# Query and key halves of the odd mixer with both input parts as one moving operand

## The chip, the core and the metric

The program runs on one core of one Trainium2 chip. Its time is the device time of one execution in microseconds (us). PE is the matmul engine, ACT the scalar engine, DVE the vector engine, POOL the GpSimd engine, SP the engine that issues the weight loads. The matmul engine's granted clock is 1.00 of its full 2.4 GHz in every stretch quoted here.

## What is computed

Three transformer-like blocks on 256 tokens of width 1024 in fp32, with a feed-forward part between the mixers. The change lies in the odd mixer, a banded attention of 16 heads of width 64:

```python
def odd_mixer(h, w_in, w_out, rel_bias):
    q, k, v = jnp.split(h @ w_in, 3, axis=-1)
    ...
    return chunk_band_attention(q, k, v, rel_bias) @ w_out
...
        s = jnp.einsum('bqhd,bkhd->bhqk', qblk.astype(jnp.float32), kb) * scale + bias[None]
        p = masked_softmax(s, valid[None, None, None, :])
        return jnp.einsum('bhqk,bkhd->bqhd', p, vb)
```

At 256 tokens a query sees its own chunk of 64 and all chunks before it, so a head's scores are one 256 x 256 matrix, kept as 128 x 128 for the first token tile and 128 x 256 for the second.

## The kernel before

fp32 products are made from two fp32r parts. A weight unit (256 columns of a weight, 128 x 2048 numbers in the buffer) is loaded by SP into one of three raw buffers; ACT writes its high part (L456, w_hi), DVE the rest (L1719, w_lo); both lie in six slots. The load of unit n waits until DVE has made the low part of unit n-3. The input, turned to have its channels on the partitions, lies in t_both as [channels, 8 k-tiles, 2 parts, 256 tokens]: t_hi and t_lo. A product is w_hi x t_hi + w_hi x t_lo + w_lo x t_hi (`three`, L1078 to L1080).

The odd mixer has 12 units of its input weight, n0 to n0+11: four for the values, which run first as pairs (`first_four`), and eight for queries and keys. Each of these eight gives two **halves** of 128 channels, one for two heads: half i belongs to group g = i // 4 of four heads, kind = i % 2 says query or key, and c = i % 4 // 2 which half of the unit. Before the change two halves of a unit (i and i+2) share a PSUM bank, 256 columns each, in banks 2 * (g % 2) + kind. ACT copies each half to q or k (L882, queries times 0.125) and counts qk_kept.

The order is written out by hand. On PE round i is: half i; at i = 8 and 12 `group_turn`, which turns the scaled output of the finished group of four heads (L1375, waits for o_ready); scores of head i-2 (L1349 and L1350, into bank 4; they wait for nmax_ok of the head before, and for POOL's padded query, L959); turn of the probabilities of head i-3 (L1358); values of head i-4 (L1366 to L1368). DVE makes the row maxima with the bias added (`maxima`, L1984), and at i = 8 and 12 `group_out`, which takes the reciprocal of the sums (L1993), multiplies (L2149) and counts o_ready. ACT makes the exponentials (`exps`, L644) and copies the turned probabilities (`keep_pt`, L636). Between these stand the splits of the weight units: `split_to(m)` makes the splits of all units below m that are still open. Every engine works through its own list in order, so an instruction that waits holds up all behind it. After the sixteen rounds `rows` multiplies with the output weight.

The feed-forward stage already has the form that the change brings to the halves: `by_channels_wide` (L1156 and L1160) takes both parts of t_both as one moving operand of 512 columns, so that w_hi x t_hi lands in the left and w_hi x t_lo in the right half of a bank, w_lo x t_hi is added to the left, and the two are added outside PE.

Of the kernel before, what the change touches and what calls it, by code (L numbers as in the profile page):

```python
# [16 lines left out]
ALU = mybir.AluOpType  # L17
ACT = mybir.ActivationFunctionType
AX = mybir.AxisListType

P = 128
S = 256
T = S // P
# [40 lines left out]
def build(nc, a, out, phases):  # L64
    stack = ExitStack()
    with stack:
# [3 lines left out]
        def sem(name):  # L70
            return stack.enter_context(nc.semaphore(name))
# [28 lines left out]
        def wv(at, *shape):  # L100
            n = int(np.prod(shape))
            v = ws[:, at:at + n]
            if len(shape) == 1:
                return v
            names = "abcd"[:len(shape)]
            return v.rearrange(f"p ({' '.join(names)}) -> p {' '.join(names)}",
                               **{c: s for c, s in zip(names, shape)})
# [35 lines left out]
        for ph in phases:  # L143
# [58 lines left out]
            else:  # L202
                q, k, v = wv(2304, 8, S), wv(4352, 8, S), wv(6400, T, D)
                bias = wv(8448, 4, 256)
                V = dict(bias=bias, q=q, k=k, o=[wv(2304 + 512 * g, T, 256) for g in range(4)])

                def reversed_bias(h, t):

# [63 lines left out]
        half_used = sem("half_used")  # L272
        last_half = sem("last_half")
        first_half_done = sem("first_half_done")
        qk_kept = sem("qk_kept")
        f_T = sem("f_T")
        dve_step = sem("dve_step")
# [107 lines left out]
        def half_of(ph, i):  # L385

            g, kind, c = i // 4, i % 2, i % 4 // 2
            return ph["n0"] + 4 + 2 * g + kind, 2 * (g % 2) + kind, g, kind, c

        ACT_CT, ACT_PE, DVE_PE = 1, 3, 2  # L390
        SINGLES = 11
# [48 lines left out]
        def _(act):  # L440
# [17 lines left out]
            def split_to(n):  # L458
                while cur[0] < min(n, N_UNITS):
                    split_hi(cur[0], widths.get(cur[0], UC))  # L460
                    cur[0] += 1
# [403 lines left out]
            def mix_odd(ph):  # L865
                V, n0 = ph["views"], ph["n0"]
                L = V["L"]
                split_to(n0 + 6)
                keep_unit(ph, 0)
                keep_unit(ph, 2)  # L870
                split_to(n0 + 7)
                keep_unit(ph, 1)
                split_to(n0 + 8)
                keep_unit(ph, 3)
                split_to(n0 + 10)
                for i in range(16):
                    n, b, g, kind, c = half_of(ph, i)
                    if c:
                        act.wait_ge(unit_used, n + 1)
                    else:  # L880
                        act.wait_ge(first_half_done, 2 * g + kind + 1)
                    nc.scalar.activation(V["qk"[kind]][:, 2 * g + c, :], bank[b][:, c * S:(c + 1) * S], ACT.Copy,  # L882
                                         scale=1.0 if kind else 0.125).then_inc(qk_kept, 1)
                    if i >= 8 and i % 4 == 0:
                        group_hi(i // 4 - 2, 6 + i // 4 % 2)
                    if i >= 3:
                        keep_pt(L, i - 3)
                    if i >= 2:
                        exps(L, i - 2)
                    if i >= 3 and i % 4 in (3, 0):  # L890
                        split_to(n0 + 11 + i // 2 - 1)
                keep_pt(L, 13)
                exps(L, 14)
                exps(L, 15)
                group_hi(2, 6)
                keep_pt(L, 14)
                keep_pt(L, 15)
                split_to(ph["after"] + 2)
                group_hi(3, 7)
                split_to(ph["after"] + 3)  # L900
# [168 lines left out]
        def _(pe):  # L1069
# [79 lines left out]
            def by_channels_wide(n, b, turn=0):  # L1149

                pe.wait_ge(lo_done, n + 1 + turn * SLOTS)
                wh, wl = w_cols(n)
                for c in range(2):
                    o, cs = bank[b + c], slice(c * P, (c + 1) * P)
                    for k in range(KT):
                        mm = nc.tensor.matmul(o[:, :], wh[:, k, cs], t_both[:, k, :, :].rearrange("p a s -> p (a s)"),  # L1156
                                              start=k == 0, stop=k == KT - 1)
                        if k == 0:
                            for j in range(KT):
                                nc.tensor.matmul(o[:, 0:S], wl[:, j, cs], t_hi[:, j, :], start=False, stop=False)  # L1160
                mm.then_inc(unit_used, 1)

            def pair_cols(w, n, k, width=UC):

# [341 lines left out]
            def mix_odd(ph):  # L1506
                V, n0 = ph["views"], ph["n0"]
                L = V["L"]
                first_four(ph, (0, 2), (1, 3))
                lo0 = seen[id(t_lo_ok)]  # L1510

                def half(i):
                    n, b, g, kind, c = half_of(ph, i)
                    pe.wait_ge(lo_done, n + 1)
                    if c:
                        pe.wait_ge(qk_kept, 4 * g + kind + 1)
                    elif g < 2:
                        pe.wait_ge(bank_free[b], ph["left"][ph["bank"].index(b)])
                    else:
                        pe.wait_ge(qk_kept, 4 * (g - 2) + 3 + kind)  # L1520
                    wh, wl = w_cols(n)
                    for k in range(KT):
                        mm = three(bank[b][:, c * S:(c + 1) * S], wh[:, k, c * P:(c + 1) * P], wl[:, k, c * P:(c + 1) * P],
                                   t_hi[:, k, :], t_lo[:, k, :], k == 0, k == KT - 1)
                    mm.then_inc(unit_used if c else first_half_done, 1)

                def scores(h):
                    pe.wait_ge(qk_kept, 4 * (h // 4) + 2 * (h % 4 // 2) + 2)
                    head_scores(L, h)

                def values(h):
                    if h >= 8 and h % 4 == 0:
                        pe.wait_ge(t_lo_ok, lo0 + h // 4 - 1)
                    head_values(L, h)

                def turn(h):
                    head_turn(L, h)

                def rows(u, t, rs=range(2)):
                    group_rows(ph, lo0, u, t, rs)  # L1540

                for i in range(16):
                    half(i)
                    if i >= 8 and i % 4 == 0:
                        group_turn(V["o"][i // 4 - 2], 6 + i // 4 % 2)
                    if i >= 2:
                        scores(i - 2)
                    if i >= 3:
                        turn(i - 3)
                    if i >= 4:  # L1550
                        values(i - 4)
                pe.wait_ge(qk_kept, 14)
                rows(0, 0, (0,))
                scores(14)
                turn(13)
                values(12)
                rows(0, 0, (1,))
                scores(15)
                values(13)
                rows(1, 0, (0,))  # L1560
                group_turn(V["o"][2], 6)
                turn(14)
                rows(1, 0, (1,))
                turn(15)
                values(14)
                pe.wait_ge(qk_kept, 16)
                rows(0, 1, (0,))
                values(15)
                rows(0, 1, (1,))
                rows(2, 0, (0,))  # L1570
                group_turn(V["o"][3], 7)
                rows(2, 0, (1,))
                rows(3, 0)
                rows(1, 1)
                rows(2, 1)
                rows(3, 1, (0,))
                turn_x(ph["next"], 0)
                rows(3, 1, (1,))
                nx(t_lo_ok, 4)
# [114 lines left out]
        def _(dve):  # L1694
# [582 lines left out]
            def mix_odd(ph):  # L2277
                V, n0 = ph["views"], ph["n0"]
                L = V["L"]

                split_to(n0 + 10)
                dve.wait_ge(bias_set, 1)
                for i in range(2, 16):
                    if i >= 8 and i % 4 == 0:
                        group_out(L, i // 4 - 2, V["o"][i // 4 - 2], 6 + i // 4 % 2)
                    maxima(L, i - 2)
                    if i >= 8 and i % 4 == 0:
                        group_lo(i // 4 - 2, 6 + i // 4 % 2)
                    if i >= 4 and i % 4 in (0, 1):
                        split_to(n0 + 11 + (i - 1) // 2 - 1)  # L2290
                group_out(L, 2, V["o"][2], 6)
                maxima(L, 14)
                maxima(L, 15)
                group_lo(2, 6)
                split_to(n0 + 17)
                group_out(L, 3, V["o"][3], 7)
                split_to(ph["after"] + 2)
                group_lo(3, 7)
                split_to(ph["after"] + 3)
# [80 lines left out]
```

## Time and profile before

| | us |
|---|---|
| median of 3 runs | 1323.35 (1323.13 to 1323.44) |
| the profiled execution | 1324.39 |
| its span | 1322.6 |
| PE busy | 1306.3 (99%) |
| DVE busy | 828.0 (63%) |
| ACT busy | 682.9 (52%) |

The profile describes one execution. Its span runs from the first to the last instruction; the time of that execution has 1.8 us more around it, and is 1.04 above the median. Times within the trace are counted from the span's start. The matmul durations that the rows give overlap, since matmuls are pipelined; the distance of two starts is what one costs.

### The profile page before, as it was taken

To read this page: it belongs to the slowest core of one execution; us is meant where nothing else is said; L and a number is where in the kernel's file an instruction comes from. 1 tells how busy PE (TensorE), PEld (TensorE's weight loads), DVE (VectorE), ACT (ScalarE), POOL (GpSimd) and SP (SyncE) were. 2 spreads that over 40 slices of the span, in tenths; PEclk is the share of its full clock that TensorE was granted. 3 is DMA by queue.
4 is the path that set the end of the run, shared out by engine and by line. 5 is a ranking of instruction groups with operands and counts; after the bars stand their busy time and mean duration, and the time that the engine had idled before them with its cause. 6 is when DMAs were issued, how large, how long until landed. Compare 5 with 4: busy or idle time off the path is not lost.

```text
span 1322.6 us, 18723 instructions
## 1 busy us (share of the span) xinstructions
PE 1306.3 (99%) x7310; PEld 1134.6 (86%) x7310; DVE 828.0 (63%) x992; ACT 682.9 (52%) x912; POOL 136.7 (10%) x162
## 2 busy tenths in 40 slices
PE   8999999999999999999999999999999999999998
PEld 7988888888888887888888888888888998888886
DVE  6997755565655558777765556665565545665553
ACT  6776544453544445556554445444454665554441
POOL 2770000000000001112100000000001441000000
PEclk9999999999999999999999999999999999999999
DMA  8334775553755545326575554675553744465540
GB/s 280 128 112 144 242 251 191 190 192 112 254 206 189 186 122 160 96 96 217 186 233 190 190 191 139 212 254 190 190 191 135 236 127 132 160 209 190 191 156 32
DMA packets 174352, 234.98 MB, mean 178 GB/s; under 512 B 4351, under 2 KB 154127, under 8 KB 174288
## 3 DMA queue, kind: packets, MB, share of 16 engines
q1 hardware_dynamic: 170368, 223.52, 50.7%
q0 software_dynamic: 3184, 9.37, 2.3%
q10 hardware_dynamic: 736, 1.19, 0.2%
q8 instruction: 45, 0.74, 0.2%
q14 instruction: 19, 0.16, 0.0%
HBM read 233.03 MB, written 1.05 MB: 177 GB/s over the span
## 4 chain that ended last, share of the span: by engine, by line
PE 92%; DVE 5%; DMA 2%; ACT 1%; issue 1%; POOL 0%; SPq 0%; DVEq 0%; ACTq 0%
PE psum L1156 22%; PE psum L1078 15%; PE psum L1080 15%; PE psum L1079 15%; PE psum L1160 12%; DVE w_lo L1719 2%; PE psum L1121 2%; PE psum L1120 2%; PE psum L1119 2%; PE psum L1350 1%; DMA raw<-in_w_in 1%; PE psum L1358 1%; PE psum L1248 1%; PE psum L1349 1%; PE psum L1367 1%; PE psum L1368 1%
## 5 line engine op out<-in xcount | busy, mean ns | idle before, releaser
L1719 DVE TENSOR_TENSOR w_lo<-raw,w_hi 128x2048 fp32r<-128x2048 f32 (+1 forms) x209 | 480.8, 2306 | 91.7 <-ACT w_hi L456 90.5
L456 ACT ACTIVATE w_hi<-raw 128x2048 fp32r<-128x2048 f32 (+1 forms) x212 | 402.6, 1905 | 40.6 <-PE psum L1080 11.2
L1156 PE MATMUL psum<-t_both,w_hi 128*128 128x512 f32 x1280 | 327.5, 393 | 0.0
L1156 PEld LDWEIGHTS psum<-t_both,w_hi 128*128 128x128 f32 x1280 | 230.2, 189 | 41.0
L1078 PE MATMUL psum<-w_hi,f_hi 128*128 128x512 f32 x488 | 192.8, 395 | 0.0
L1080 PE MATMUL psum<-w_hi,f_lo 128*128 128x512 f32 x488 | 190.2, 390 | 0.0
L1079 PE MATMUL psum<-w_lo,f_hi 128*128 128x512 f32 x488 | 190.1, 389 | 0.0
L1160 PEld LDWEIGHTS psum<-t_both,w_lo 128*128 128x128 f32 x1280 | 174.6, 190 | 12.3
L1160 PE MATMUL psum<-t_both,w_lo 128*128 128x256 f32 x1280 | 178.5, 282 | 0.0
L1078 PE MATMUL psum<-w_hi,t_both 128*128 128x512 f32 (+2 forms) x464 | 167.4, 361 | 2.8 <-DVE g_row L1959 2.7
L1080 PE MATMUL psum<-w_hi,t_both 128*128 128x512 f32 (+2 forms) x464 | 163.1, 351 | 0.0
L1079 PE MATMUL psum<-w_lo,t_both 128*128 128x512 f32 (+2 forms) x464 | 162.9, 351 | 0.0
L558 ACT ACTIVATE ws<-psum 128x512 f32<-128x512 f32 x40 | 24.0, 599 | 259.7 <-PE psum L1156 259.7
L1882 DVE TENSOR_TENSOR ws<-psum,ws 128x512 f32<-128x512 f32 x40 | 27.7, 692 | 199.6 <-ACT ws L558 199.6
L929 POOL TENSOR_TENSOR st<-st,minus_half 128x1 f32<-128x1 f32 (+3 forms) x35 | 27.3, 779 | 1016.6 <-DVE st L1766 756.4
L1080 PEld LDWEIGHTS psum<-w_hi,f_lo 128*128 128x128 f32 x488 | 91.6, 188 | 19.3
L1079 PEld LDWEIGHTS psum<-w_lo,f_hi 128*128 128x128 f32 x488 | 91.7, 188 | 18.1
L1078 PEld LDWEIGHTS psum<-w_hi,f_hi 128*128 128x128 f32 x488 | 91.7, 188 | 18.1
L1078 PEld LDWEIGHTS psum<-w_hi,t_both 128*128 128x128 f32 x464 | 88.4, 191 | 15.7 <-DVE g_row L1959 3.1
L1080 PEld LDWEIGHTS psum<-w_hi,t_both 128*128 128x128 f32 x464 | 88.4, 190 | 11.7
L1079 PEld LDWEIGHTS psum<-w_lo,t_both 128*128 128x128 f32 x464 | 88.6, 191 | 10.5
L1078 PE MATMUL psum<-t_both,w_hi 128*128 128x256 f32 x192 | 55.6, 290 | 1.4 <-ACT ws L882 0.8
(190 smaller groups left out, 1473.8 us busy)
## 6 DMA issues: line engine op xcount, KB each, us to landing
raw<-in_ffn_wg SPq DMA_DIRECT2D x44, 1024.0 KB, 5.5
raw<-in_ffn_wu SPq DMA_DIRECT2D x44, 1024.0 KB, 5.2
raw<-in_ffn_wd SPq DMA_DIRECT2D x44, 1024.0 KB, 5.0
raw<-in_even_w_in SPq DMA_DIRECT2D x12, 1024.0 KB, 5.1
raw<-in_odd_w_in SPq DMA_DIRECT2D x12, 1024.0 KB, 5.3
raw<-in_w_gate SPq DMA_DIRECT2D x11, 1024.0 KB, 5.5
raw<-in_w_up SPq DMA_DIRECT2D x11, 1024.0 KB, 5.3
raw<-in_w_down SPq DMA_DIRECT2D x11, 1024.0 KB, 4.9
```

Source lines behind the costliest of these rows:

```text
L456: nc.scalar.activation(w_hi[:, n % SLOTS, 0:w], raw[:, n % RAWS, 0:w], ACT.Copy).then_inc(hi_done, 1)
L929: nc.gpsimd.tensor_tensor(v, v, minus_half[:, 0:1].broadcast_to([P, v.shape[1]]), ALU.pow).then_inc(rstd_ready, 1)
L1078: nc.tensor.matmul(o, lh, rh, start=start, stop=False)
L1079: nc.tensor.matmul(o, lh, rl, start=False, stop=False)
L1080: return nc.tensor.matmul(o, ll, rh, start=False, stop=stop)
L1119: nc.tensor.matmul(out, t_hi[:, k, ts], wh(k), start=k == 0, stop=False)
L1120: nc.tensor.matmul(out, t_lo[:, k, ts], wh(k), start=False, stop=False)
L1121: return lambda: [nc.tensor.matmul(out, t_hi[:, k, ts], wl(k), start=False, stop=k == KT - 1) for k in range(KT)]
L1156: mm = nc.tensor.matmul(o[:, :], wh[:, k, cs], t_both[:, k, :, :].rearrange("p a s -> p (a s)"), start=k == 0, stop=k == KT - 1)
L1160: nc.tensor.matmul(o[:, 0:S], wl[:, j, cs], t_hi[:, j, :], start=False, stop=False)
L1719: nc.vector.tensor_tensor(w_lo[:, n % SLOTS, 0:w], raw[:, n % RAWS, 0:w], w_hi[:, n % SLOTS, 0:w].bitcast(F32), ALU.subtract).then_inc(lo_ ...
L1882: nc.vector.tensor_tensor(halves(f_s[:, b, :]), halves_of(4)[0], f_b[:, 0, :, :], ALU.add).then_inc(gate_sum, 1)
```

## The change

`half` on PE no longer calls `three` for each of eight k-tiles on 256 columns. It calls the new `by_channels_half`, which is the body of `by_channels_wide` for one c: one matmul of 512 columns with w_hi over t_both for k = 0, then eight of 256 columns with w_lo over t_hi, then seven more of 512. The half now fills a whole bank, so half i uses bank i % 4. Halves 0 to 3 wait for the bank to be left by the values; from half 4 on they wait for half i-4 to be kept.

ACT no longer writes q or k. It copies the right half of the bank into one of two buffers of 256 columns (in `masks`, whose tables aren't needed any more) and counts qk_part; from i = 2 on it waits until DVE has used that buffer. DVE adds: `whole(i)` waits for qk_part, takes the left half of the bank times 0.125 or 1 plus the buffer, writes q or k and counts qk_kept.

The weight splits at the start move. ACT made those of n0+8 and n0+9 before round 0, and makes them after the copies of halves 0 and 1. DVE made those up to n0+9 before the first maxima; now that of n0+7 stands behind the sum of half 0, that of n0+8 behind the sum of half 2, that of n0+9 behind the sum of half 3.

```diff
@@ half_of
-            return ph["n0"] + 4 + 2 * g + kind, 2 * (g % 2) + kind, g, kind, c
+            return ph["n0"] + 4 + 2 * g + kind, i % 4, g, kind, c
@@ ACT, mix_odd
-                split_to(n0 + 10)
                 for i in range(16):
...
-                    nc.scalar.activation(V["qk"[kind]][:, 2 * g + c, :], bank[b][:, c * S:(c + 1) * S], ACT.Copy,
-                                         scale=1.0 if kind else 0.125).then_inc(qk_kept, 1)
+                    if i >= 2:
+                        act.wait_ge(qk_kept, i - 1)
+                    nc.scalar.activation(V["part"][:, i % 2, :], bank[b][:, S:2 * S], ACT.Copy, scale=1.0 if kind else 0.125).then_inc(qk_part, 1)
+                    if i < 2:
+                        split_to(n0 + 9 + i)
@@ PE
+            def by_channels_half(n, b, c):
+
+                wh, wl = w_cols(n)
+                o, cs = bank[b], slice(c * P, (c + 1) * P)
+                for k in range(KT):
+                    mm = nc.tensor.matmul(o[:, :], wh[:, k, cs], t_both[:, k, :, :].rearrange("p a s -> p (a s)"),
+                                          start=k == 0, stop=k == KT - 1)
+                    if k == 0:
+                        for j in range(KT):
+                            nc.tensor.matmul(o[:, 0:S], wl[:, j, cs], t_hi[:, j, :], start=False, stop=False)
+                return mm
@@ PE, mix_odd, half
-                    if c:
-                        pe.wait_ge(qk_kept, 4 * g + kind + 1)
-                    elif g < 2:
+                    if i < 4:
                         pe.wait_ge(bank_free[b], ph["left"][ph["bank"].index(b)])
                     else:
-                        pe.wait_ge(qk_kept, 4 * (g - 2) + 3 + kind)
-                    wh, wl = w_cols(n)
-                    for k in range(KT):
-                        mm = three(bank[b][:, c * S:(c + 1) * S], wh[:, k, c * P:(c + 1) * P], wl[:, k, c * P:(c + 1) * P],
-                                   t_hi[:, k, :], t_lo[:, k, :], k == 0, k == KT - 1)
-                    mm.then_inc(unit_used if c else first_half_done, 1)
+                        pe.wait_ge(qk_kept, i - 3)
+                    by_channels_half(n, b, c).then_inc(unit_used if c else first_half_done, 1)
@@ DVE, mix_odd
-                split_to(n0 + 10)
+                def whole(i):
+
+                    n, b, g, kind, c = half_of(ph, i)
+                    dve.wait_ge(qk_part, i + 1)
+                    nc.vector.scalar_tensor_tensor(out=V["qk"[kind]][:, 2 * g + c, :], in0=bank[b][:, 0:S], scalar=1.0 if kind else 0.125,
+                                                   in1=V["part"][:, i % 2, :], op0=ALU.mult, op1=ALU.add).then_inc(qk_kept, 1)
+
+                split_to(n0 + 7)
+                whole(0)
+                split_to(n0 + 8)
+                whole(1)
                 dve.wait_ge(bias_set, 1)
                 for i in range(2, 16):
+                    whole(i)
+                    if i < 4:
+                        split_to(n0 + 7 + i)
                     if i >= 8 and i % 4 == 0:
                         group_out(L, i // 4 - 2, V["o"][i // 4 - 2], 6 + i // 4 % 2)
                     maxima(L, i - 2)
```

DVE's list at the start of the odd mixer, from the last instruction of the stage before (L1805), before the change. The names: w_lo is a split, ws,st<-psum,ws the maxima of one token tile, and each is followed by a short read of its accumulator.

```order
L1805 TENSOR_TENSOR t_both<-psum,t_both 128x4x128 [waits t_hi_ok] x2
L1719 TENSOR_TENSOR w_lo<-raw,w_hi 128x2048 [waits hi_done] x6
L1984 ISA ws,st<-psum,ws 128x128 [waits bias_in0,s_done,bias_set]
L1984 ISA st 128x1
L1984 ISA ws,st<-psum,ws 128x256
L1984 ISA st 128x1
```

The same place after the change; ws<-psum,masks is the sum of a half.

```order
L1721 TENSOR_TENSOR w_lo<-raw,w_hi 128x2048 [waits hi_done] x3
L2287 SCALAR_TENSOR_TENSOR ws<-psum,masks 128x256 [waits qk_part]
L1721 TENSOR_TENSOR w_lo<-raw,w_hi 128x2048 [waits hi_done]
L2287 SCALAR_TENSOR_TENSOR ws<-psum,masks 128x256 [waits qk_part]
L2287 SCALAR_TENSOR_TENSOR ws<-psum,masks 128x256 [waits qk_part,bias_set]
L1721 TENSOR_TENSOR w_lo<-raw,w_hi 128x2048 [waits hi_done]
L1986 ISA ws,st<-psum,ws 128x128 [waits bias_in0,s_done]
L1986 ISA st 128x1
L1986 ISA ws,st<-psum,ws 128x256
L1986 ISA st 128x1
L2287 SCALAR_TENSOR_TENSOR ws<-psum,masks 128x256 [waits qk_part]
L1721 TENSOR_TENSOR w_lo<-raw,w_hi 128x2048 [waits hi_done]
```

The block of six splits ahead of the first maxima is broken up. Sums of halves 0 to 3 stand in it, and the last two splits stand each between a sum and the maxima of heads 0 and 1.

DVE's list around round 8, before the change: L1993 and L2149 are the output of the first group.

```order
L1984 ISA ws,st<-psum,ws 128x128 [waits bias_in1,p_done,s_done]
L1984 ISA st 128x1
L1984 ISA ws,st<-psum,ws 128x256
L1984 ISA st 128x1
L1993 RECIPROCAL st<-st 128x8 [waits o_done]
L2149 TENSOR_TENSOR ws<-psum,st 128x512 [waits dve_step]
L1984 ISA ws,st<-psum,ws 128x128 [waits bias_in2,p_done,s_done]
```

The same place after the change (L1995 and L2151 are those two).

```order
L1986 ISA ws,st<-psum,ws 128x128 [waits bias_in1,p_done,s_done]
L1986 ISA st 128x1
L1986 ISA ws,st<-psum,ws 128x256
L1986 ISA st 128x1
L2287 SCALAR_TENSOR_TENSOR ws<-psum,masks 128x256 [waits qk_part]
L1995 RECIPROCAL st<-st 128x8 [waits o_done]
L2151 TENSOR_TENSOR ws<-psum,st 128x512 [waits dve_step]
L1986 ISA ws,st<-psum,ws 128x128 [waits bias_in2,p_done,s_done]
```

The output of the group stood behind the maxima of head 5 alone, and now the sum of half 8 stands between them.

PE's list at the end of half 8, before the change: the group's turn is L1375.

```order
L1078 MATMUL psum<-t_both,w_hi 128x256
L1079 MATMUL psum<-t_both,w_hi 128x256
L1080 MATMUL psum<-t_both,w_lo 128x256
L1375 MATMUL psum<-ident,ws 128x128 [waits o_ready]
L1375 MATMUL psum<-ident,ws 128x128 x3
L1349 MATMUL psum<-ws 128x128 [waits qz_ok,nmax_ok,qk_kept]
L1350 MATMUL psum<-ws 128x256
L1358 MATMUL psum<-ident,ws 128x128 [waits pt_kept,p_done]
```

And after it, where the turn is L1383:

```order
L1164 MATMUL psum<-t_both,w_hi 128x512 [waits qk_kept,lo_done]
L1168 MATMUL psum<-t_both,w_lo 128x256 x8
L1164 MATMUL psum<-t_both,w_hi 128x512 x7
L1383 MATMUL psum<-ident,ws 128x128 [waits o_ready]
L1383 MATMUL psum<-ident,ws 128x128 x3
L1357 MATMUL psum<-ws 128x128 [waits qz_ok,nmax_ok,qk_kept]
L1358 MATMUL psum<-ws 128x256
L1366 MATMUL psum<-ident,ws 128x128 [waits pt_kept,p_done]
```

The turn of the group keeps its place behind half 8, with its wait for o_ready; the half has become sixteen matmuls.

## Rows read from the trace of the kernel before

**Rows 1.** The page: chain that ended last, by engine.

```profile
PE 92%; DVE 5%; DMA 2%; ACT 1%; issue 1%; POOL 0%; SPq 0%; DVEq 0%; ACTq 0%
```

**Rows 2.** Stretch of the halves: us, then PE, PEld, DVE, ACT, POOL busy (instructions).

```profile
1033.17:1097.90 64.73, 63.95 (x523) 62.53 (x522) 30.94 (x67) 39.42 (x87) 29.88 (x43) 1.00 0.58 176
```

**Rows 3.** Waits, 1033 to 1098 us: waiter <- releaser, total, times, longest.

```profile
PE psum L1078 <- ACT ws L882: 0.8, 1, 0.8
```

**Rows 4.** Timeline of PE, halves 0 to 2: start us, us, engine, line, operation.

```profile
1033.17 0.28 PE L1078 MATMUL psum<-t_both,w_hi 128*128 128x256 f32 x1
...
1038.80 0.28 PE L1080 MATMUL psum<-t_both,w_lo 128*128 128x256 f32 x1
1039.87 0.36 PE L1078 MATMUL psum<-t_both,w_hi 128*128 128x256 f32 x1 [0.78 <-ACT ws L882]
```

**Rows 5.** Chain of waits, feed-forward stage (L1121 its pair products): start us, us.

```profile
1135.56 1.81 PE psum L1121 x8
...
1161.49 0.95 PE psum L1160 x8
1162.44 1.84 PE psum L1156 x8
```

**Rows 6.** Timeline of ACT, opening.

```profile
1037.54 1.91 ACT L456 ACTIVATE w_hi<-raw 128x2048 fp32r<-128x2048 f32 x1 [1.77 <-DMA raw<-in_odd_w_in]
1039.36 0.64 ACT L882 ACTIVATE ws<-psum 128x256 f32<-128x256 f32 x2
```

**Rows 7.** Timeline of DVE: two splits back to back.

```profile
1023.15 4.50 DVE L1719 TENSOR_TENSOR w_lo<-raw,w_hi 128x2048 fp32r<-128x2048 f32 x2 [1.01 <-ACT w_hi L456]
```

**Rows 8.** L2026, the nearest operation to the sum: duration ns min/median/max.

```profile
L2026 DVE SCALAR_TENSOR_TENSOR ws<-psum,p_col,ws x4: 470/474/485, 28.1 to 40.5; 128x256 f32<-128x256 f32 x4
```

**Rows 9.** Timeline of all engines, round 7.

```profile
1063.78 0.39 PE L1349 MATMUL psum<-ws 128*128 128x128 f32 x2
...
1063.97 0.38 ACT L882 ACTIVATE ws<-psum 128x256 f32<-128x256 f32 x1 [2.18 <-PE psum L1080]
...
1064.63 0.29 DVE L1984 CUSTOM_DVE_ANT_0 ws<-psum,ws 128x128 f32<-128x128 f32 x1 [3.88 <-PE psum L1350]
...
1065.19 0.08 DVE L1984 DVE_READ_ACCUMULATOR2_ANT st<- 128x1 f32 x1
...
1065.35 0.40 ACT L644 ACTIVATE ws<-ws,st 128x128 f32<-128x128 f32 x1
...
1066.13 0.19 ACT L644 ACTIVATION_READ_ACCUMULATOR ws<-ws,st 128x1 f32 x1
```

**Rows 10.** Timeline of PE, rounds 2 to 4.

```profile
1042.82 0.39 PE L1349 MATMUL psum<-ws 128*128 128x128 f32 x2
...
1043.29 0.47 PE L1078 MATMUL psum<-t_both,w_hi 128*128 128x256 f32 x1
...
1046.34 0.39 PE L1349 MATMUL psum<-ws 128*128 128x128 f32 x2
...
1051.77 0.36 PE L1078 MATMUL psum<-t_both,w_hi 128*128 128x256 f32 x1
```

**Rows 11.** Timeline of all engines, half 8: group output, its turn, the copy.

```profile
1065.35 0.36 PE L1078 MATMUL psum<-t_both,w_hi 128*128 128x256 f32 x1
...
1065.58 0.20 DVE L1993 RECIPROCAL st<-st 128x8 f32<-128x8 f32 x1 [0.30 <-PE psum L1368]
...
1065.82 0.69 DVE L2149 TENSOR_TENSOR ws<-psum,st 128x512 f32<-128x512 f32 x1
...
1068.30 0.60 PE L1375 MATMUL psum<-ident,ws 128*128 128x128 f32 x4
1068.49 0.38 ACT L882 ACTIVATE ws<-psum 128x256 f32<-128x256 f32 x1 [0.37 <-PE psum L1080]
```

**Rows 12.** Timeline of all engines, a DVE result that PE waits for.

```profile
1118.90 0.69 DVE L2159 TENSOR_TENSOR t_both<-psum,t_both 128x512 fp32r<-128x512 f32 x1 [0.78 <-ACT t_both L863]
...
1119.65 0.50 PE L1078 MATMUL psum<-w_hi,t_both 128*128 128x512 f32 x1
```

**Rows 13.** The page, DMA issues: KB each, us to landing.

```profile
raw<-in_odd_w_in SPq DMA_DIRECT2D x12, 1024.0 KB, 5.3
```

**Rows 14.** Timeline of POOL: the first padded query.

```profile
1039.82 2.76 POOL L959 TENSOR_SCALAR ws<-ws,st 128x256 f32<-128x256 f32 x1 [17.68 <-ACT ws L882]
```

More of the change, by code:

```diff
@@ L204, in build @@
                 bias = wv(8448, 4, 256)
-                V = dict(bias=bias, q=q, k=k, o=[wv(2304 + 512 * g, T, 256) for g in range(4)])
+                V = dict(bias=bias, q=q, k=k, part=masks[:, :].rearrange("p (a s) -> p a s", a=2), o=[wv(2304 + 512 * g, T, 256) for g in range(4)])
                 def reversed_bias(h, t):
@@ L274, in build @@
         first_half_done = sem("first_half_done")
+        qk_part = sem("qk_part")
         qk_kept = sem("qk_kept")
@@ L1151, in by_channels_wide @@
                 pe.wait_ge(lo_done, n + 1 + turn * SLOTS)
+                for c in range(2):
+                    mm = by_channels_half(n, b + c, c)
+                mm.then_inc(unit_used, 1)
+            def by_channels_half(n, b, c):
                 wh, wl = w_cols(n)
-                for c in range(2):
-                    o, cs = bank[b + c], slice(c * P, (c + 1) * P)
-                    for k in range(KT):
[L1156 to L1161, printed above, removed]
+                o, cs = bank[b], slice(c * P, (c + 1) * P)
[6 more added lines that the diff above has]
+                return mm
             def pair_cols(w, n, k, width=UC):
@@ L1514, in half @@
                     pe.wait_ge(lo_done, n + 1)
-                    if c:
-                        pe.wait_ge(qk_kept, 4 * g + kind + 1)
-                    elif g < 2:
+                    if i < 4:
                         pe.wait_ge(bank_free[b], ph["left"][ph["bank"].index(b)])
                     else:
-                        pe.wait_ge(qk_kept, 4 * (g - 2) + 3 + kind)
-                    wh, wl = w_cols(n)
-                    for k in range(KT):
-                        mm = three(bank[b][:, c * S:(c + 1) * S], wh[:, k, c * P:(c + 1) * P], wl[:, k, c * P:(c + 1) * P],
-                                   t_hi[:, k, :], t_lo[:, k, :], k == 0, k == KT - 1)
-                    mm.then_inc(unit_used if c else first_half_done, 1)
+                        pe.wait_ge(qk_kept, i - 3)
+                    by_channels_half(n, b, c).then_inc(unit_used if c else first_half_done, 1)
                 def scores(h):
```

## Prediction

> **What bounds the kernel now.** I read the page's chain of waits first: 92% of the chain that ended last is PE, so time won or lost on PE counts in full, and time on another engine counts only where PE waits for it [rows 1]. Then the stretches: from 1033.17 to 1097.90 us, where the sixteen query and key halves run, PE is busy for 63.95 of 64.73 us at full clock, DVE for 30.94 and ACT for 39.42 [rows 2]. Then the waits: PE has exactly one there, 0.8 us, for the ACT copy of L882 [rows 3]. So the stage is bound by PE's own stream. Two questions follow: what the new stream costs, and whether the longer way out of PSUM (ACT copy, then DVE sum, in place of one ACT copy) reaches PE. I call half i's end the start of the next PE instruction after it.
>
> **PE stream, halves.** A half is now 24 matmuls of 256 columns. The first starts at 1033.17, the second half's last at 1038.80, to which one more distance of 0.12 comes, so two halves take 5.75 us, 2.875 each [rows 4]. The new half is eight of 512 and eight of 256, as the feed-forward stage runs them: in the chain eight of 512 take 1.84 us and eight of 256 take 0.95, 2.79 together [rows 5]. The gain is 0.085 a half, 16 x 0.085 = 1.4 us. The columns are equal before and after. A third of the instructions goes, and one of 512 at 230 ns against two of 256 at 119.8 each is the whole difference. The nearest cheaper row for 512 columns is that of L1121, eight in 1.81, 226 ns each [rows 5]; that would make 2.76 and 1.8 us. Dearest is no gain at all, 0. I take 1.4, as the same instruction sequence stands in the chain.
>
> The Trainium skill (TensorE: Matmul & The Clock Gate, Back-to-back issue gap) gives about 131 ns for a 512-column matmul in a sustained stream of weight loads and matmuls. The rows have 230 ns in just such a stream and speak against it; the sum goes by the row, and by the page it would be lower by 8 x 0.099 x 16 = 12.7 us.
>
> **The wait removed.** Half 2 shares a bank with half 0 today and may start only when ACT has copied half 0. ACT is then behind its weight split of 1037.54, which itself waited 1.77 us for a DMA, so the copy comes at 1039.36 and PE's matmul at 1039.87 instead of 1038.92: 0.95 us lost [rows 4, 6]. With banks by i % 4, half 2 takes a bank long free and this goes. Half 2 then starts at 33.17 + 2 x 2.79 = 1038.75 and ends at 1041.54, where it ended at 1042.82. Gain so far 1.28.
>
> **What is late next: the opening.** DVE no longer makes all splits before the loop: the one of unit n0+8 comes between the sum of half 2 and the maxima of head 0, that of n0+9 between the sum of half 3 and the maxima of head 1. Two splits take DVE 4.50 us, so one holds it 2.2 [rows 7]; the sum, an operation of 256 columns from PSUM and SBUF, takes 0.47 [rows 8], and the maxima 0.65 (1064.63 to 1065.27) [rows 9]. Half 2 ends 41.54; ACT copy starts 0.19 later and is done after 0.38 (+0.03) [rows 9], so 42.14; sum to 42.6, with the split issued at about 42.53 and over at 44.74; maxima to 45.40. Half 3 starts after head 0's scores (0.47 [rows 10]) at 42.01 and takes 3.05 - 0.085 (1043.29 to 1046.34 today [rows 10]), to 44.98. But the scores of head 1 overwrite the score bank and wait for those maxima: PE stands 0.42. They start at 45.40 where they started at 46.34 [rows 10]. Then the turn of head 0 needs its exponentials, done some 0.95 after the maxima (1065.35 to 1066.32 [rows 9]), 46.35, while PE is there at 46.05: 0.30 more. Half 4 starts when the turn has run for 0.25, at 46.60, and takes 2.95 - 0.085 (1065.35 to 1068.30 for half 8 today [rows 11]), to 49.47. Meanwhile ACT, in order, does part 3 only after those exponentials (46.28 to 46.7), DVE sums to 47.1, splits to 49.29, and the maxima of head 1 are ready at 49.95: the scores of head 2 wait 0.48, its turn again 0.30, and half 5 begins at about 1051.83 against 1051.77 [rows 10]. The opening thus loses 0.42 + 0.30 + 0.48 + 0.30 = 1.5 and wins 0.95 + 5 x 0.085 = 1.38, net +0.1. Bounds: with a sum of 0.4 instead of 0.47 the losses are 1.35; if the lag is not caught up while units n0+10 and n0+11 are split, two or three more waits of 0.3 to 0.6 follow, so 1.2 to 3.
>
> **The inner loop, halves 5 to 15.** The maxima of head i-2 stand behind the sum of half i. The sum ends 0.19 + 0.38 + 0.03 + 0.47 = 1.07 after the half; DVE can issue the next at 1.0. Today the maxima start 0.85 after it (1064.63 against 1063.78) [rows 9], so they and the exponentials come 0.15 later. PE's turn of that head comes only in the next round, 4.5 us on, and needs the exponentials, which then end 2.7 us after the half's end (1066.32 less 1063.78, plus 0.15) [rows 9]: covered by some 2.4 us. DVE's load rises to at most 0.4 + 0.65 + 2.2 of 4.5 us, and ACT's is unchanged. Cost nothing; gain 11 x 0.085 = 0.93.
>
> **Two group turns.** Here the price lies. At i = 8 and 12 PE turns the finished group of four heads right after the half (1068.30, L1375), waiting for o_ready. Today DVE made that group's scaled output long before: the reciprocal at 1065.58 and the product at 1065.82, during half 8, 1.8 us ahead of need [rows 11]. In the new order the sum of half i stands in front of it on DVE, and the sum needs the half to be finished. So PE ends half 8 and then waits for copy, sum, reciprocal and product: 0.19 + 0.38 + 0.03, then 0.40 until DVE issues the next, 0.93 from the reciprocal's start to the product's end (1066.51 less 1065.58) [rows 11], and 0.06 from DVE's end to PE's start (1119.59 to 1119.65) [rows 12]: 1.99 us. Nothing covers it, as scores, turn and values stand behind the group turn on PE. Twice: +3.98. A longer stall would need ACT late for the copy; it runs a split before half 8's copy, and its row at 1068.49 shows 0.37 us of idle time between them [rows 11], of which 0.15 is used. Bounds 1.8 to 2.3 each. The third and fourth group outputs come after the loop, with no sum in front.
>
> **Small edits.** The weight splits made later also let DMAs start later (the load of n0+10 waits for the low part of n0+7, 39.2 instead of 34.9); each lands in 5.3 us [rows 13] and is wanted at 48 us or later: nothing. POOL's first padded query took 2.76 us beside a split of DVE [rows 14]; pad 0 starts with a split at 36.9, ends by 40, and is wanted at 41.54: nothing. The buffer for the parts is memory no longer read. Semaphores: no instruction of their own.
>
> **Sum.** +0.1 (opening) - 0.93 + 3.98 = +3.1 us. The profiled execution has 1324.39 us with a span of 1322.6, 1.0 above the median; its successor should show about 1327.5 and 1325.7. On the median: 1323.35 + 3.1 = 1326.4.
>
> **Rivals.** First, milder waits: a group turn costs 1.8, the opening's waits are half of 1.5, and the 512-column pace is 226 ns, so that a half gains 0.115. Opening 0.75 - 0.95 - 5 x 0.115 = -0.8, halves 5 to 15 -1.25, turns +3.6: +1.6, or 1325.0, no change that can be told. For it: the opening's waits are differences of 0.3 to 0.5 between long chains. Against: the turns' wait is a plain chain of measured rows.
>
> Second, the lag that isn't caught up: ACT does copy, exponentials and split strictly in order, and a late copy delays the sum, and that the next maxima. If units n0+10 and n0+11 (1.9 us each on ACT) hold it up through halves 4 to 7, 1.5 to 2.5 us come on top: 1328.4. For it: in a round with a split ACT has only 0.37 us spare [rows 11]. Against: rounds without one leave it 2.18 [rows 9], and three of them follow.
>
> Third, the other side: the wide matmul is cheaper than the row. It decides where 16 halves win 4.5 us instead of 1.4: 0.28 each, a half of 2.59, (2.59 - 0.95) / 8 = 205 ns for 512 columns. At 190 ns a half takes 2.47, the halves win 6.5 and the sum is -2.0, 1321.3. Against: no row of this trace is under 226 ns.
>
> The page's rule on sustained streams, named above, is the far end of this rival: by its 131 ns the forecast would be 1313.7. That the change doesn't do what it says is ruled out by the order of instructions, which has the 512-column form in all sixteen halves.
>
> **How the numbers follow.** Forecast 1326.4: 0.62. Milder: 0.20. Lag: 0.13. Other side: 0.05, of which the 131 ns 0.01. The range, 1324.6 to 1328.6, takes the forecast's bounds (opening -0.2 to +1.6, turns 3.6 to 4.6, halves -1.7 to 0) and most of the two nearer rivals, and leaves some 0.15 out. A measurement of this kernel tells about 0.2%, 2.65 us, from no change, so 1326.0 is the border of slower: the forecast lies only 0.4 above it. Of the forecast's 0.62 I give 0.48 to above it, of the lag all: slower 0.61. Same: 0.14 + 0.20 + 0.02 of the third = 0.36. Faster: the rest of the third, 0.03.
>
> **What would show it.** PE must have two idle stretches of about 2 us, before the group turns at some 1069.6 and 1089.8, released by DVE's product; four small ones of 0.3 to 0.5 in 1045 to 1051 before scores and turns; none before half 2. Eight 512-column matmuls in a half take 1.84. The maxima of heads 0 and 1 stand behind a split. If PE shows no wait at the group turns, the prediction's main step is wrong; if waits go on past half 6, the second rival holds.

## The result, and the profile after

| | before | after |
|---|---|---|
| median, us (20 runs each) | 1322.91 (1320.74 to 1324.0) | 1326.07 (1324.05 to 1327.38) |
| ratio to before | | 1.0026, 95% interval 1.002 to 1.0032 |
| profiled execution, us | 1324.39 | 1327.38 |
| its span, us | 1322.6 | 1325.6 |
| start of half 0 in it, us | 1033.17 | 1032.84 |
| from there to the end of the span, us | 289.4 | 292.8 |

The kernel became 3.2 us slower, a quarter of a per cent, and the interval lies clear of 1; 1326.4 had been forecast, from 1323.35. In the following the last line of the table is the measure within a trace: what lies ahead of the odd mixer varied by 2.4 us between the profiled executions of all these kernels (half 0 starts between 1030.8 and 1033.2), with no instruction changed there. What lies behind half 15 took 221.7 us in all nine traces, so the differences arise within the halves. By this measure the change cost 3.3 us. Spans are printed to 0.1 us, and such a difference is good to about 0.1.

The page of the changed kernel, sections 1 and 4:

```profile
PE 1304.4 (98%) x7182; PEld 1125.5 (85%) x7182; DVE 833.2 (63%) x1008; ACT 683.9 (52%) x912; POOL 139.1 (10%) x162
...
PE 90%; DVE 6%; issue 1%; DMA 1%; ACT 1%; POOL 0%; DVEq 0%; ACTq 0%; POOLq 0%
```

PE's share of the chain fell from 92% [rows 1] to 90%, though PE is still the engine that sets the end: it is now held at places by DVE. The waits of PE in the odd mixer (waiter <- releaser: total, times, longest) name them:

```profile
PE psum L1383 <- DVE ws L2151: 3.5, 2, 1.8
PE psum L1357 <- issue: 0.7, 2, 0.4
```

The wait for the ACT copy [rows 3] is gone. In its place stand two waits for the group output L2151, and two before scores (L1357) that the profile calls issue, which means that it names no releaser. Two more, before turns, show only in the weight loads of the turn (PEld):

```profile
PEld psum L1366 <- ACT ws L645: 1.0, 2, 0.5
```

**The stream.** The first matmul of half 0 in the timeline of PE, from which the table counts:

```profile
1032.84 0.39 PE L1164 MATMUL psum<-t_both,w_hi 128*128 128x512 f32 x1
```

And the chain through halves 0 to 2 (start us, us):

```profile
1034.18 1.84 PE psum L1164 x8
1036.02 0.95 PE psum L1168 x8
1036.97 1.84 PE psum L1164 x8
1038.81 0.95 PE psum L1168 x8
```

1036.97 less 1034.18 is 2.79 us a half, against 2.875 before [rows 4], and the same two numbers as in the feed-forward stage [rows 5].

**The opening.** Timeline of all engines, rounds 2 and 3 (start us, us, engine, line, operation, idle before):

```profile
1041.22 0.38 PE L1357 MATMUL psum<-ws 128*128 128x128 f32 x2
...
1041.42 0.38 ACT L884 ACTIVATE masks<-psum 128x256 f32<-128x256 f32 x1 [0.60 <-PE psum L1164]
...
1041.90 0.42 DVE L2287 SCALAR_TENSOR_TENSOR ws<-psum,masks 128x256 f32<-128x256 f32 x1 [2.44 <-ACT masks L884]
...
1042.24 2.28 DVE L1721 TENSOR_TENSOR w_lo<-raw,w_hi 128x2048 fp32r<-128x2048 f32 x1
...
1044.44 0.28 DVE L1986 CUSTOM_DVE_ANT_0 ws<-psum,ws 128x128 f32<-128x128 f32 x1
...
1045.12 0.40 ACT L645 ACTIVATE ws<-ws,st 128x128 f32<-128x128 f32 x1 [2.01 <-DVE st L1986]
...
1045.18 0.46 PE L1357 MATMUL psum<-ws 128*128 128x128 f32 x2 [0.36 <-issue]
...
1046.15 0.55 PE L1366 MATMUL psum<-ident,ws 128*128 128x128 f32 x3
...
1049.79 0.46 PE L1357 MATMUL psum<-ws 128*128 128x128 f32 x2 [0.29 <-issue]
...
1051.73 0.47 PE L1164 MATMUL psum<-t_both,w_hi 128*128 128x512 f32 x1
```

Read it downwards: half 2 ends at 1041.22, ACT copies, DVE adds (L2287), and then DVE splits a weight unit (L1721) for 2.28 us while the scores of head 0 lie finished. The maxima (L1986) begin at 1044.44 and the next scores at 1045.18. PE stands before them, then before the turn at 1046.15, for the exponentials (L645), and again at both places in the round after.

**The group turn.** Timeline of all engines around the end of half 8:

```profile
1068.13 0.38 ACT L884 ACTIVATE masks<-psum 128x256 f32<-128x256 f32 x1 [0.22 <-PE psum L1164]
1068.55 0.42 DVE L2287 SCALAR_TENSOR_TENSOR ws<-psum,masks 128x256 f32<-128x256 f32 x1 [3.47 <-ACT masks L884]
1068.89 0.19 DVE L1995 RECIPROCAL st<-st 128x8 f32<-128x8 f32 x1
1069.12 0.69 DVE L2151 TENSOR_TENSOR ws<-psum,st 128x512 f32<-128x512 f32 x1
...
1069.86 0.66 PE L1383 MATMUL psum<-ident,ws 128*128 128x128 f32 x4 [1.77 <-DVE ws L2151]
...
1070.35 0.39 PE L1357 MATMUL psum<-ws 128*128 128x128 f32 x2
```

The output of the group, made during half 8 before [rows 11], now follows copy and sum. The last matmul of half 8 starts at 1067.70, so the half ends at some 1067.94; the turn starts at 1069.86, 1.92 us later. The second one, at 1090.08, shows the same 1.77 us of idle time.

### The profile page after: what moved, and what is told of

The parts are those of the page before. It is cut to its first block, busy times and chain, and to the rows that moved or that the text cites. A ratio compares the mean times of both kernels' runs of the same rounds, so it can differ in the third digit from the quotient of the medians.

```text
span 1325.6 us, 18498 instructions
## 1 busy us (share of the span) xinstructions
PE 1304.4 (98%) x7182; PEld 1125.5 (85%) x7182; DVE 833.2 (63%) x1008; ACT 683.9 (52%) x912; POOL 139.1 (10%) x162
## 4 chain that ended last, share of the span: by engine, by line
PE 90%; DVE 6%; issue 1%; DMA 1%; ACT 1%; POOL 0%; DVEq 0%; ACTq 0%; POOLq 0%
PE psum L1164 24%; PE psum L1081 14%; PE psum L1083 14%; PE psum L1082 14%; PE psum L1168 13%; DVE w_lo L1721 2%; PE psum L1124 2%; PE psum L1123 2%; PE psum L1122 2%; PE psum L1358 1%; PE psum L1256 1%; PE psum L1366 1%; PE psum L1357 1%; PE psum L1375 1%; PE psum L1376 1%
## 5 line engine op out<-in xcount | busy, mean ns | idle before, releaser
L1721 DVE TENSOR_TENSOR w_lo<-raw,w_hi 128x2048 fp32r<-128x2048 f32 (+1 forms) x209 | 480.9, 2306 | 88.0 <-ACT w_hi L457 86.8
L1164 PE MATMUL psum<-t_both,w_hi 128*128 128x512 f32 x1408 | 363.0, 393 | 0.0
L1164 PEld LDWEIGHTS psum<-t_both,w_hi 128*128 128x128 f32 x1408 | 253.3, 189 | 44.6
L1168 PEld LDWEIGHTS psum<-t_both,w_lo 128*128 128x128 f32 x1408 | 192.1, 190 | 13.1
L1168 PE MATMUL psum<-t_both,w_lo 128*128 128x256 f32 x1408 | 196.2, 282 | 0.0
L962 POOL TENSOR_SCALAR ws<-ws,st 128x256 f32<-128x256 f32 x32 | 35.3, 1105 | 115.1 <-PE psum L1358 66.7
```

The lines of the kernel that those rows point to most:

```text
L962: nc.gpsimd.tensor_scalar(L["qz"][h % 2], L["q2"](h), st[:, 60 + h % 2:61 + h % 2], None, ALU.mult).then_inc(qz_ok, 1)
L1721: nc.vector.tensor_tensor(w_lo[:, n % SLOTS, 0:w], raw[:, n % RAWS, 0:w], w_hi[:, n % SLOTS, 0:w].bitcast(F32), ALU.subtract).then_inc(lo_ ...
```

## Experiments

Two theories were held against each other. The first: all of the loss is the order on DVE's queue, at two group turns (3.9 us) and in the opening (1.5), while the form of the halves itself gains. The rival: the wide form, or the longer way out of PSUM, costs PE time through all sixteen halves. In the table "stage" is half 0's start to the end of the span.

| kernel | half 0 at | span | stage | less before | ratio, 95% interval |
|---|---|---|---|---|---|
| before | 1033.17 | 1322.6 | 289.4 | | |
| changed | 1032.84 | 1325.6 | 292.8 | +3.3 | 1.0026 (1.002 to 1.0032) |
| e1_group_first | 1033.24 | 1322.0 | 288.8 | -0.7 | 0.9997 (0.9988 to 1.0006) |
| e2_splits_behind | 1031.90 | 1322.9 | 291.0 | +1.6 | 1.0014 (1.0005 to 1.0023) |
| e3_both | 1033.18 | 1320.3 | 287.1 | -2.3 | 0.9982 (0.9973 to 0.9991) |
| e4_parts_apart | 1031.12 | 1324.8 | 293.7 | +4.3 | 1.0038 (1.0024 to 1.0051) |
| e5_banks_only | 1032.16 | 1321.4 | 289.2 | -0.2 | 1.0001 (0.9992 to 1.001) |
| e6_turn_late | 1030.84 | 1323.4 | 292.6 | +3.1 | 1.0028 (1.0017 to 1.0038) |
| e8_banks_early_copy | 1032.27 | 1320.6 | 288.3 | -1.1 | 0.9993 (0.9984 to 1.0003) |

### e1_group_first: the group output back ahead of the sum

```diff
                 for i in range(2, 16):
+                    if i >= 8 and i % 4 == 0:
+                        group_out(L, i // 4 - 2, V["o"][i // 4 - 2], 6 + i // 4 % 2)
                     whole(i)
                     if i < 4:
                         split_to(n0 + 7 + i)
-                    if i >= 8 and i % 4 == 0:
-                        group_out(L, i // 4 - 2, V["o"][i // 4 - 2], 6 + i // 4 % 2)
                     maxima(L, i - 2)
```

> The changed kernel with one thing moved back: in rounds 8 and 12 DVE makes the group's scaled output ahead of the sum of that round's half, as it could before the change. Theory (order on DVE's queue): both waits of 1.9 us before the group turns vanish, PE keeps four small waits of 0.3 to 0.5 us in the opening; 3.9 us less than the changed kernel, 0.6 to 0.8 us under the kernel before, ratio to it about 0.9995. Rival (the wide form or the longer way out of PSUM costs PE time through all halves): the waits move or shrink, and the time stays within 1 us of the changed kernel, ratio 1.0015 or more.

Its stage is 4.0 us shorter than the changed kernel's. PE's waits in the odd mixer:

```profile
PE psum L1357 <- issue: 0.6, 2, 0.4
```

Both waits for L2151 are gone and the small ones stand as they were. So the two turns cost more than the whole net loss of 3.3 us, and without them the change gains 0.7 us by the stage, which the ratio's interval can't tell from nothing.

### e2_splits_behind: two splits behind the maxima

```diff
                     whole(i)
-                    if i < 4:
-                        split_to(n0 + 7 + i)
                     if i >= 8 and i % 4 == 0:
                         group_out(L, i // 4 - 2, V["o"][i // 4 - 2], 6 + i // 4 % 2)
                     maxima(L, i - 2)
+                    if i < 4:
+                        split_to(n0 + 7 + i)
```

> The changed kernel with DVE's splits of units n0+8 and n0+9 behind the maxima of heads 0 and 1 in place of ahead of them. Theory: the four waits before scores and turns in 1045 to 1051 us vanish, 1.5 to 1.8 us; the two group turns still wait 1.9 us each. So +1.6 us on the kernel before, ratio 1.0012. Rival (ACT in order is what holds the opening up): the waits stay though the splits have moved, ratio still 1.0025.

1.8 us less than the changed kernel, at the upper end of what was expected. The waits of PE that are left:

```profile
PE psum L1383 <- DVE ws L2151: 3.5, 2, 1.8
```

Nothing before scores or the turns of the probabilities remains, with ACT's list unchanged. What held up the opening was the split in front of the maxima, not ACT.

### e3_both: both moves

The diffs of e1_group_first and e2_splits_behind together.

> Both moves at once: group output ahead of the sum, and the two splits behind the maxima. Theory: PE has no wait over 0.1 us in the sixteen rounds; what is left are the two gains, 0.95 us for the wait before half 2 and 16 x 0.085 us for the form of the halves: 2.2 us under the kernel before, ratio 0.9983. Rival (the waits hide one another, or others come up): above 0.9993.

The two savings add up, 4.0 + 1.8 against 5.6 to 5.7 measured. No wait of PE in the sixteen rounds is left in its trace. The group output lies again well before its turn:

```profile
1063.89 0.20 DVE L1995 RECIPROCAL st<-st 128x8 f32<-128x8 f32 x1 [0.21 <-PE psum L1376]
...
1064.13 0.69 DVE L2151 TENSOR_TENSOR ws<-psum,st 128x512 f32<-128x512 f32 x1
...
1066.55 0.60 PE L1383 MATMUL psum<-ident,ws 128*128 128x128 f32 x4
1066.74 0.38 ACT L884 ACTIVATE masks<-psum 128x256 f32<-128x256 f32 x1 [0.23 <-PE psum L1164]
...
1067.16 0.42 DVE L2287 SCALAR_TENSOR_TENSOR ws<-psum,masks 128x256 f32<-128x256 f32 x1 [2.34 <-ACT masks L884]
```

At 0.9982 it is the fastest kernel of this study, 2.4 us under the kernel before (1320.93 against 1323.36, medians measured side by side). Its stage gains 2.3 of the 2.3 that the form (1.4) and the wait before half 2 (0.95) come to.

### e4_parts_apart: six of eight k-tiles as two matmuls of 256 columns

```diff
                     for k in range(KT):
-                        mm = nc.tensor.matmul(o[:, :], wh[:, k, cs], t_both[:, k, :, :] ..., start=k == 0, stop=k == KT - 1)
+                        if k == 0 or k == KT - 1:
+                            mm = nc.tensor.matmul(bank[b][:, :], wh[:, k, cs], t_both[:, k, :, :] ..., start=k == 0, stop=k == KT - 1)
+                        else:
+                            nc.tensor.matmul(bank[b][:, 0:S], wh[:, k, cs], t_hi[:, k, :], start=False, stop=False)
+                            nc.tensor.matmul(bank[b][:, S:2 * S], wh[:, k, cs], t_lo[:, k, :], start=False, stop=False)
```

> The changed kernel, with six of the eight 512-column matmuls of each half as two of 256 columns, high part to the left and low part to the right of the bank; all else (banks, copies, sums, queues) as changed. Theory: a half costs 6 x (2 x 119.8 - 230) ns = 0.06 us more, 16 halves 0.92, of which the waits of the opening hide some 0.1: +0.8 us on the changed kernel, ratio to the kernel before 1.0030. Rival (512 columns cost no less than two of 256): no change against the changed kernel.

0.9 to 1.0 us over the changed kernel in the stage, and 1.0038 against 1.0026 in the ratio, whose intervals overlap. By the stage the 512-column form is worth what the rows said, some 10 ns for each pair of matmuls joined; the interval alone would not carry it.

### e5_banks_only: half i in bank i % 4, in the kernel before

```diff
-            return ph["n0"] + 4 + 2 * g + kind, 2 * (g % 2) + kind, g, kind, c
+            return ph["n0"] + 4 + 2 * g + kind, i % 4, g, kind, c
...
-                    if c:
-                        pe.wait_ge(qk_kept, 4 * g + kind + 1)
-                    elif g < 2:
+                    if i < 4:
                         pe.wait_ge(bank_free[b], ph["left"][ph["bank"].index(b)])
                     else:
-                        pe.wait_ge(qk_kept, 4 * (g - 2) + 3 + kind)
+                        pe.wait_ge(qk_kept, i - 3)
```

> The kernel before with one part of the change alone: half i in bank i % 4 (left 256 columns), PE waiting from half 4 on for half i-4 to be kept; three matmuls of 256 columns per k-tile, one ACT copy and all splits as before. Theory: the wait before half 2 goes, 0.95 us, and nothing comes up: from the first half's start to the end of the span 288.5 us in place of 289.4, ratio 0.9993. Rival (the late ACT copy just holds up the scores of head 0 instead, through POOL's padded query): the wait moves to the first L1349 and less than 0.4 us is won.

Here the rival was right and the theory wrong. PE no longer waits before half 2, and waits before the first scores instead:

```profile
PE psum L1349 <- POOL ws L959: 0.7, 1, 0.7
```

The timeline of all engines shows why:

```profile
1038.30 0.64 ACT L882 ACTIVATE ws<-psum 128x256 f32<-128x256 f32 x2
...
1038.43 2.29 DVE L1717 TENSOR_TENSOR w_lo<-raw,w_hi 128x2048 fp32r<-128x2048 f32 x1 [1.35 <-ACT w_hi L456]
...
1038.77 2.75 POOL L959 TENSOR_SCALAR ws<-ws,st 128x256 f32<-128x256 f32 x1 [17.65 <-ACT ws L882]
...
1041.66 0.46 PE L1349 MATMUL psum<-ws 128*128 128x128 f32 x2 [0.72 <-POOL ws L959]
```

POOL pads the query of head 0 only after ACT's copy of half 0, which is late behind a split that waited for its DMA; POOL's 256 columns then take 2.75 us beside DVE's split, and PE is there first. A bank of its own alone wins 0.1 to 0.2 us by the stage.

### e6_turn_late: the wait at the group turns, in the kernel before

```diff
                     if i >= 8 and i % 4 == 0:
+                        dve.wait_ge(qk_kept, i + 1)
                         group_out(L, i // 4 - 2, V["o"][i // 4 - 2], 6 + i // 4 % 2)
```

> The kernel before, with one wait added: in rounds 8 and 12 DVE makes the group's output only after that round's half has been copied to q or k by ACT. No sum, no wide matmul, all splits as before. Theory: PE waits before each group turn for copy (0.19 + 0.38 + 0.03), reciprocal to product (0.93) and 0.06: 1.6 us, twice, +3.2 us, ratio 1.0024. That is the changed kernel's wait less the sum's 0.4. Rival (the wait at the turns is due to the sum or the wide form): no wait, ratio 1.0000.

+3.1 us by the stage, with no sum, no wide matmul and no other edit. Its waits of PE:

```profile
PE psum L1375 <- DVE ws L2149: 2.9, 2, 1.4
PE psum L1078 <- ACT ws L882: 0.6, 1, 0.6
```

The second line is the wait before half 2 that the kernel before has too. 1.44 us of idle time before each turn, against 1.77 with the sum in between: the order alone makes four fifths of the wait, and the sum the rest.

### e8_banks_early_copy: the banks, and the copy of half 0 ahead of a split

e5_banks_only, and on ACT:

```diff
-                split_to(n0 + 10)
+                split_to(n0 + 9)
                 for i in range(16):
...
                                          scale=1.0 if kind else 0.125).then_inc(qk_kept, 1)
+                    if i == 0:
+                        split_to(n0 + 10)
```

> The banks-only kernel, with ACT's split of unit n0+9 behind the copy of half 0 in place of ahead of it. Theory (the wait had moved to the scores of head 0, since POOL's padded query began only after the late copy and then ran 2.75 us beside a DVE split): the copy comes 0.2 us after half 0, POOL is done by 1039, and PE has no wait in the opening; from the first half's start to the end of the span 0.95 us less than the kernel before, 288.5 us, ratio 0.9993. Rival (POOL is the bound there however early the copy is): the wait before the first L1349 stays above 0.4 us.

-1.1 us by the stage, and no wait of PE in the odd mixer; the ratio's interval just reaches 1. POOL and ACT in its opening:

```profile
1035.34 0.38 ACT L882 ACTIVATE ws<-psum 128x256 f32<-128x256 f32 x1 [0.47 <-PE psum L1082]
...
1035.83 2.17 POOL L961 TENSOR_SCALAR ws<-ws,st 128x256 f32<-128x256 f32 x1 [14.59 <-ACT ws L882]
...
1038.55 0.36 ACT L882 ACTIVATE ws<-psum 128x256 f32<-128x256 f32 x1
...
1040.90 0.39 PE L1351 MATMUL psum<-ws 128*128 128x128 f32 x2
```

The copy starts at 1035.34 and the padded query is ready at 1038.00, 2.9 us ahead of the scores. So the 0.95 us of the removed wait needs ACT's copy ahead of its split. Whether it needs the bank as well was not tested, and this trace speaks against it: the copy of half 0 is over at 1035.72, 2.3 us before half 2 starts (1032.27 + 5.75 = 1038.02), and that of half 1 (1038.55) well before half 3 at 1041.37, so PE would find a shared bank copied in time. A run of the kernel before with the early copy alone was not made.

With e3_both it also prices the form by itself: both kernels have banks of their own, an early copy and no wait of PE, and their stages differ by 1.2 us, against the 1.4 of 16 x 0.085.

## Why the prediction held

**The stream** was right: 2.79 us a half in the chain, 16 x 0.085 = 1.4 us. e4_parts_apart gives 0.9 to 1.0 for six eighths of it, e3_both against e8_banks_early_copy 1.2 for all of it.

**The wait removed** was right in size, 0.95: half 2 ends at 1041.22, 8.38 us after half 0's start, where 8.37 had been forecast. The reason was told too narrowly. The text forecast rightly that POOL's padded query would be done by 40 (it is at 1039.67), but put the gain down to the banks alone. e5_banks_only shows that the banks alone only hand the wait on to the scores of head 0, through POOL, and e8_banks_early_copy that ACT's copy of half 0 ahead of a split, which is part of the same change, is what it takes; whether the banks matter at all here stays open.

**The opening** was forecast at a net +0.1 us. Half 5 starts 18.89 us after half 0 (1051.73 less 1032.84), before 18.60 (1051.77 less 1033.17 [rows 4, 10]): +0.3. The four waits are at the four places named, and 0.2 us larger in sum. The scores of head 1 come 12.34 us after half 0's start, where 12.23 had been forecast. The chain left out the step from the end of the maxima on DVE to PE's scores (1045.08 to 1045.18, 0.10 us), though it counted 0.06 for the like step at the group turns. "Semaphores: no instruction of their own" was not quite right either: the sum of half 2 waits for two, the chain shows a step L2286 for the wait, and the sum starts 0.10 us after the copy's end in place of 0.03. e2_splits_behind shows that this item is worth 1.8 us where 1.5 was forecast, and that its cause is the split ahead of the maxima.

**Halves 5 to 15** cost nothing, as forecast: between the two group turns PE has no wait, and DVE's sum in front of the maxima stays hidden in the round.

**The group turns** were forecast at 1.99 each and took 1.92; e1_group_first takes them away, 4.0 us, and e6_turn_late makes them in the kernel before. The step was right in cause, place and size.

Sum: +0.3 - 0.9 + 3.8, and 0.1 for the turn after a wait, which takes 0.49 (1069.86 to 1070.35) in place of 0.43, twice: 3.3 us, the stage's difference. The median's 3.2 agrees with it. That the total comes within 0.2 us of the forecast's 3.1 is in part that the opening cost 0.2 more and the two turns 0.1 less. The forecast's bounds, added up, would end at 1329.6 (1.6 + 4.6 on 1323.35), above the range's 1328.6; the measured time is far from either.

**The rivals.** The milder case (+1.6) needed the opening's waits at half their size; they came out larger. The lag that is not caught up didn't come: no wait after half 5 but the two. The third, a cheaper wide matmul, is out: the halves of the changed kernel take the 230 ns per 512 columns of [rows 5]. The Trainium skill's figure of about 131 ns for a sustained stream (TensorE: Matmul & The Clock Gate, Back-to-back issue gap) is not met by any row of this case.

## What to carry to other kernels

When a result gets a second step on another engine, look in that engine's written order for what now stands behind the new step, and who waits for it: work that was done early out of idle time is moved behind a result that comes late, and an engine that idles half of its time can still cost 2 us at each such place. Put what depends only on older data (here the group output) ahead of the new wait, and long work that nobody awaits (a weight split) behind the short work that somebody does. And a wait taken off the critical engine is won only if whatever the same late result feeds is early too: here another bank alone won next to nothing, and ACT's copy made early with it won the whole.

## What the runs showed of the hardware

An operation of POOL on 128 x 256 fp32 took 0.91 to 0.94 us alone, and 0.92 beside the maxima of DVE, which read PSUM and SBUF (1060.52 in the changed kernel). When it started within DVE's split, which reads two SBUF tensors, it ended 0.8 us after the split did, however much of the split was left. Of the changed kernel, all engines:

```profile
1036.59 2.28 DVE L1721 TENSOR_TENSOR w_lo<-raw,w_hi 128x2048 fp32r<-128x2048 f32 x1
...
1036.78 2.89 POOL L962 TENSOR_SCALAR ws<-ws,st 128x256 f32<-128x256 f32 x1 [14.96 <-DVE ws L2287]
...
1042.24 2.28 DVE L1721 TENSOR_TENSOR w_lo<-raw,w_hi 128x2048 fp32r<-128x2048 f32 x1
1042.75 2.57 POOL L962 TENSOR_SCALAR ws<-ws,st 128x256 f32<-128x256 f32 x1
```

1036.78 + 2.89 = 1039.67 against the split's end at 1038.87, and 1045.32 against 1044.52; in e5_banks_only 1041.52 against 1040.72. Where it started 0.36 us ahead of a split (1053.34 against 1053.70 in the changed kernel) it took its 0.92 us all the same, and 0.93 where it started 0.24 ahead (1046.50 against 1046.74); there the split took 2.39 us in place of 2.28. So POOL made nearly no headway under a split that had begun, and wasn't held up by one that began 0.24 us after it. A start 0.05 us ahead took 3.05 us, in e2_splits_behind (1041.81) and in e3_both (1043.09); between 0.05 and 0.24 there is no row. The Trainium skill (GPSIMD Engine Reference, 1. Specifications) has the two engines contend where DVE has two SBUF inputs; these rows agree and give it a size.
